# Two weight tiles moved ahead of modulation blocks in the load queue at the start of a two-block transformer kernel

## What is computed

```python
mod = jax.nn.silu(c) @ w_ada[l] + b_ada[l]
sh1, sc1, g1, sh2, sc2, g2 = jnp.split(mod[:, None, :], N_MOD, axis=-1)
u = rmsnorm(h, norm1_w[l]) * (1.0 + sc1) + sh1
proj = u @ w_in[l]
hq, hf, hi, hg, aq, ak, av = jnp.split(proj, offs, axis=-1)
o_hg = hgrn2(hq, hf, hi, hg, lower_bounds[l], hgrn_gnorm_w[l])
lam = (exp(sum(diff_lambda_q1 * diff_lambda_k1)) - exp(sum(diff_lambda_q2 * diff_lambda_k2)) + lambda_init)
o_da = diff_attention(aq, ak, av, lam, lambda_init, diff_subln_w[l])
mix = jnp.concatenate([o_hg, o_da], axis=-1) @ w_out[l]
h = h + g1 * mix
u = rmsnorm(h, norm2_w[l]) * (1.0 + sc2) + sh2
h = h + g2 * ((jax.nn.silu(u @ w_ffn_gate[l]) * (u @ w_ffn_up[l])) @ w_ffn_down[l])
```

## Time and profile before

| what | value |
|---|---|
| median of 3 runs | 1474.66 us |
| the profiled execution | 1473.02 us |
| its span, first to last instruction | 1471.2 us |
| around the span | 1.8 us |
| PE busy, share of the span | 98% |
| DVE busy | 64% |
| ACT busy | 28% |
| granted TensorE clock, mean | 0.991 |

### The profile page before, as it was taken

How to read it: one execution, slowest core, us unless ns; L and a number is a source line. 1 busy time by engine, 2 the same in 40 slices (tenths; PEclk the granted TensorE clock), 3 DMA queues, 4 the chain that set the end, 5 groups by cost and what they waited for, 6 DMA issues and landing times.

```text
span 1471.2 us, 19416 instructions
## 1 busy us (share of the span) xinstructions
PE 1445.6 (98%) x7240; PEld 1174.3 (80%) x7240; DVE 937.3 (64%) x1666; ACT 412.9 (28%) x838; POOL 94.9 (6%) x75
## 2 busy tenths in 40 slices
PE   8999999999999999999999999999999999999997
PEld 7888777778888888888877777788887888888886
DVE  8887797886676665566566668765565444544443
ACT  6335355231111111013345456410122222221011
POOL 0100000200000001225100000000120000000110
PEclk9999999999999999999999999999999999999998
DMA  9444421436556564533221111123322232233332
GB/s 369 183 158 141 146 77 51 149 130 206 187 191 194 186 195 138 159 93 116 74 71 44 44 51 42 46 93 101 101 85 93 93 99 101 86 100 93 95 96 89
DMA packets 52464, 175.26 MB, mean 119 GB/s; under 512 B 5936, under 2 KB 6320, under 8 KB 52400
## 3 DMA queue, kind: packets, MB, share of 16 engines
q1 hardware_dynamic: 52400, 174.41, 36.0%
HBM read 172.29 MB, written 2.10 MB: 119 GB/s over the span
## 4 chain that ended last, share of the span: by engine, by line
PE 91%; DVE 4%; DMA 1%; ACT 1%; issue 1%; SPq 0%; ACTq 0%; DVEq 0%
PE bank L669 20%; PE bank L671 20%; PE bank L670 20%; PE bank L1182 8%; PE bank L1202 2%; PE bank L1237 2%; PE bank L1213 2%; PE bank L1036 2%; PE bank L861 2%; PE bank L863 2%; PE bank L862 2%; DMA fraw<-in_w_in_dram 1%; PE bank L895 1%; PE bank L834 1%; PE bank L835 1%
## 5 line engine op out<-in xcount | busy, mean ns | idle before, releaser
L669 PE MATMUL bank<-uh,wh 128*128 128x512 f32 x808 | 316.7, 392 | 6.1 <-DVE wl L1736 4.5
L670 PE MATMUL bank<-ul,wh 128*128 128x512 f32 x808 | 315.5, 390 | 0.0
L671 PE MATMUL bank<-uh,wl 128*128 128x512 f32 x808 | 315.5, 390 | 0.0
L1734 DVE CAST wh<-wraw 128x1024 fp32r<-128x1024 f32 (+1 forms) x223 | 147.8, 663 | 194.4 <-PE bank L671 178.8
L1736 DVE TENSOR_TENSOR wl<-wraw,wh 128x1024 fp32r<-128x1024 f32 (+1 forms) x223 | 261.4, 1172 | 7.7
L669 PEld LDWEIGHTS bank<-uh,wh 128*128 128x128 f32 x808 | 152.4, 189 | 38.9 <-issue 5.8
L671 PEld LDWEIGHTS bank<-uh,wl 128*128 128x128 f32 x808 | 152.4, 189 | 32.1
L670 PEld LDWEIGHTS bank<-ul,wh 128*128 128x128 f32 x808 | 152.5, 189 | 31.6
L669 PE MATMUL bank<-hh,wh 128*128 128x512 f32 x352 | 137.5, 391 | 0.0
L671 PE MATMUL bank<-hh,wl 128*128 128x512 f32 x352 | 137.0, 389 | 0.0
L670 PE MATMUL bank<-hl,wh 128*128 128x512 f32 x352 | 137.0, 389 | 0.0
(11 more groups left out here) (362 smaller groups left out, 2263.3 us busy)
## 6 DMA issues: line engine op xcount, KB each, us to landing
ada<-in_w_ada_dram SPq DMA_DIRECT2D x94, 512.0 KB, 4.7
wraw<-in_w_in_dram SPq DMA_DIRECT2D x61, 512.0 KB, 3.4
wraw<-in_w_ffn_gate_dram SPq DMA_DIRECT2D x44, 512.0 KB, 3.4
wraw<-in_w_ffn_up_dram SPq DMA_DIRECT2D x44, 512.0 KB, 3.4
wraw<-in_w_ffn_down_dram SPq DMA_DIRECT2D x32, 512.0 KB, 3.5
wraw<-in_w_ffn_down_dram SPq DMA_DIRECT2D x16, 384.0 KB, 3.1
wraw<-in_w_out_dram SPq DMA_DIRECT2D x16, 256.0 KB, 2.7
wraw<-in_w_out_dram SPq DMA_DIRECT2D x8, 512.0 KB, 3.4
```

The lines of the kernel that those rows point to most:

```text
L669: nc.tensor.matmul(bank[:], a, rh[:, k0 + k, :], start=(first and k == 0), stop=False)
L670: nc.tensor.matmul(bank[:], a, rl[:, k0 + k, :], start=False, stop=False)
L671: mm = nc.tensor.matmul(bank[:], b, rh[:, k0 + k, :], start=False, stop=(last and k == nk - 1))
L1734: V.tensor_copy(wh[:, slot, 0:n], wraw[:, slot, 0:n]).then_inc(w_hi, 1)
```

## The change

On SP the eight front units are issued in three groups, two behind the modulation blocks of k = 0, four behind those of k = 1, two behind those of k = 2; the lambda row and the second vector go behind all modulation blocks. On DVE the rests of units 4 and 5 stand at the end of k = 1's rests, those of units 6 and 7 behind `front_low(2)`, in each case ahead of `x_normed` and `front_gain`; the small chains of k = 3 and k = 6 stand behind the level masks, and on both sides of the late modulation blocks. On ACT the exponentials go behind the loop. PE's and POOL's order is unchanged.

```diff
+        FRONT_UNITS = [(0, 1), (2, 3, 4, 5), (6, 7)] + [()] * (KT - 3)
...
             for k in range(KT):
                 load_front_mod(2 * k)
                 load_front_mod(2 * k + 1)
-                if k < FRONT // 2:
-                    load_front_unit(2 * k)
-                    load_front_unit(2 * k + 1)
-                if k == 1:
-                    sp.dma_start(lamv[:].rearrange("p a d -> p (a d)"),
-                                 t_in["lam"].broadcast_to([P, 4 * HD])).then_inc(lam_in, 16)
-                if k == 4:
-                    sp.dma_start(vt2[:], t_in["vec_2"]).then_inc(vec_in, 16)
+                for n in FRONT_UNITS[k]:
+                    load_front_unit(n)
+            sp.dma_start(lamv[:].rearrange("p a d -> p (a d)"),
+                         t_in["lam"].broadcast_to([P, 4 * HD])).then_inc(lam_in, 16)
+            sp.dma_start(vt2[:], t_in["vec_2"]).then_inc(vec_in, 16)
             sp.dma_start(scb[:, 1, :], t_in["c_2"].broadcast_to([P, D])).then_inc(c_land, 16)
...
             for k in range(KT):
-                if k == 5:
-                    act.wait_ge(setup_v, 5)
-                    A(lsc[:, 4:12], lsc[:, 4:12], ACT.Exp)
-                    A(lsc[:, 20:22], lsc[:, 20:22], ACT.Exp).then_inc(setup_a, 1)
...
                 A(uh[:, k, :], tn[:, k % 4], ACT.Copy).then_inc(n_uh, 1)
+            act.wait_ge(setup_v, 5)
+            A(lsc[:, 4:12], lsc[:, 4:12], ACT.Exp)
+            A(lsc[:, 20:22], lsc[:, 20:22], ACT.Exp).then_inc(setup_a, 1)
...
             for k in range(1, KT):
+                if k == 1:
+                    front_rest(2)
+                    front_rest(3)
                 if k < FRONT // 2:
-                    front_rest(2 * k)
-                    front_rest(2 * k + 1)
                     front_low(k)
+                if 0 < k < FRONT // 2 - 1:
+                    front_rest(2 * k + 2)
+                    front_rest(2 * k + 3)
                 for n in (2 * k, 2 * k + 1):
                     if n < KT:
                         x_normed(n)
...
-                if k == 3:
-                    l0, l1 = vt1[:, LB:LB + 4], vt1[:, LB + 4:LB + 8]
...
-                if k == 6:
-                    v.wait_ge(setup_a, 1)
...
             level_masks(range(5, 7))
+            l0, l1 = vt1[:, LB:LB + 4], vt1[:, LB + 4:LB + 8]
...
+            v.wait_ge(lam_in, 16)
...
             for j in range(16, MOD0):
                 late_modulation(j)
+            v.wait_ge(setup_a, 1)
...
             v.wait_ge(mod_done, MOD0)
```

More of the change, by code:

```diff
@@ L1989, in _ @@
-            level_masks(range(5, 7))
+            level_masks(range(5, 7))
+            l0, l1 = vt1[:, LB:LB + 4], vt1[:, LB + 4:LB + 8]
+            link(V.tensor_tensor(lsc[:, 0:4], l0, l1, ALU.max))
+            link(V.tensor_tensor(lsc[:, 4:8], l0, lsc[:, 0:4], ALU.subtract))
+            link(V.tensor_tensor(lsc[:, 8:12], l1, lsc[:, 0:4], ALU.subtract))
+            v.wait_ge(lam_in, 16)
+            for m in range(2):
+                link(V.tensor_tensor_reduce(lamv[:, 2 * m, :], lamv[:, 2 * m, :], lamv[:, 2 * m + 1, :], 1.0, 0.0,
+                                            ALU.mult, ALU.add, lsc[:, 20 + m:21 + m]))
@@ L1990, in _ @@
             for j in range(16, MOD0):
                 late_modulation(j)
+            v.wait_ge(setup_a, 1)
+            link(V.tensor_tensor(lsc[:, 12:16], lsc[:, 4:8], lsc[:, 8:12], ALU.add))
+            link(V.reciprocal(lsc[:, 16:20], lsc[:, 12:16]))
+            link(V.tensor_tensor(lbs, lsc[:, 4:8], lsc[:, 16:20], ALU.mult))
+            link(V.tensor_scalar(oml, lbs, -1.0, 1.0, ALU.mult, ALU.add))
+            link(V.tensor_tensor(lsc[:, 22:23], lsc[:, 20:21], lsc[:, 21:22], ALU.subtract))
@@ L1992, in _ @@
+            link(V.tensor_scalar(nlam, lsc[:, 22:23], LAMBDA_INIT, -1.0, ALU.add, ALU.mult))
             v.wait_ge(mod_done, MOD0)
```

## The result

| | before | after |
|---|---|---|
| median, us | 1473.3 (22 runs, 1470.87 to 1480.75) | 1477.74 (22 runs, 1475.98 to 1479.72) |
| ratio to before | | 1.0028, 95% interval 1.0021 to 1.0034 |
| profiled execution, us | 1473.02 | 1478.43 |
| its span, us | 1471.2 | 1475.9 |

The change makes the kernel 4.1 us slower, 3.1 to 5.0 by the interval.

What follows compares the result with a forecast made beforehand. TensorE, busy 98% of the span, was taken as the bound, with VectorE deciding the front. 1.9 us at unit 7 plus 0.9 for the clock gave +2.8, added to the median: 1477.5 us, range 1472.5 to 1481.0.

Steps and rivals of the forecast that it cites:

- Where the front's delay goes: Front of the kernel: a delay of TensorE there reaches the end almost one to one.
- Units 4 and 5 earlier, the pause goes: Front loads: units 4 and 5 land at 20.2 and 21.4, and TensorE's 2.08 us pause for unit 4's rest goes.
- VectorE stands for 1.6 us behind each gain: VectorE in the front: after the gains of k = 2 and 3 it idles about 1.6 us until `ul` can start.
- +1.9 us at unit 7: TensorE begins unit 7 at 40.7 instead of 38.84, waiting for VectorE's eighth `xn`: +1.9 us.
- +0.9 us for the clock: Low TensorE clock behind the new pause at unit 7: between 0 and 1.7 us, the middle taken, +0.9 us.
- The rest, at nothing: Lambda and lower-bound chains and exponentials moved behind the loop: 0 us, VectorE through at 64.8, hidden by the `forget` wait.
- lambda row too late: Rival behind the loop: ScalarE and VectorE wait for the late-issued lambda row, +8 us or more; chance 0.03.
- Absorbed: Rival: later waits of TensorE, such as those for VectorE, take up the delay, 0 us; chance 0.09.
- no stall: Rival in the front: VectorE's 1.7 us hops are hidden after all and unit 7 begins at 37.3, -1.5 us; chance 0.07.
- Late all the same: Rival: the slow DMA stretch is not the lambda row's, unit 4 is rounded at 24.2, +4.8 us; chance 0.11.
- The possible gain: TensorE's front pause and low clock: 3.8 us at most; VectorE's chain without a stall gives only -1.5 us.

Runs made afterwards that it cites:

- rests back in their places: The changed kernel with VectorE's rests of units 2k and 2k+1 again ahead of the `ul` of k, loads as changed: 1472.52 us, ratio 0.9998.
- half of the column sums: 16 of TensorE's 32 column-sum matmuls left out, as a time probe, in three kernels: before 1471.21 us, changed 1475.65, VectorE in order of need 1470.15.
- filled pauses: The changed kernel with 7 and 14 zero-weight matmuls put into TensorE's two pauses (third `ul`, unit 7): 1475.46 us, ratio 1.0017 to before.
- interleaved order: The changed kernel with VectorE's `xn`, unit rests and gains in the order in which TensorE needs them: 1472.76 us, ratio 1.0001 to before.
- order alone: The kernel before with only VectorE's new order of unit rests; loads, lambda chains and ScalarE as they were: 1480.55 us, ratio 1.0049.

## Why the prediction was right, and where it was off

The predicted 1477.5 us stand against 1477.74 measured, in the range of 1472.5 to 1481.0. The direction and the place were right. But the sum was 2.8 us and the measured difference is 4.1 (3.1 to 5.0). The two errors, the sum and the median of three to which it was added (1.4 us too high), cancelled: that the number came out this near is luck, the place and the way are not.

- *Where the front's delay goes.* Almost one to one to the end, as said. Over all 14 profiles the next phase begins between 65.94 and 77.30 us, and what is left of the span behind that lies between 1401.0 and 1403.2 us.
- *Units 4 and 5 earlier, the pause goes.* Shown. ScalarE rounded unit 4 at 21.92 (forecast 21.35; its work before that was 0.6 us late by the column sums). Unit 4 landed at 21.7, though, not at 20.2: issued at 7.48 and 14.2 us on its way. With ScalarE not free before 21.9 this cost nothing here. With the rests back in their places ScalarE did wait for it, 0.29 us.
- *VectorE stands for 1.6 us behind each gain.* Shown: 1.54 us twice, 0.26 for unit 6 (forecast 0.4). With half of the column sums, where nothing comes late at the start, the changed kernel follows the forecast's times: third gain 28.61 (28.4), third `ul` 30.31 (30.1), end of the eighth `xn` 40.85 (40.7), unit 7 at 40.99 (40.7).
- *+1.9 us at unit 7: too small.* Against that one execution it is right (41.67 - 38.84, less 0.9 for the column sums). The step that failed is the base of 38.84. It was taken from an execution in which TensorE itself was late, by the pause of 2.08 us and the low clock behind it. Without that, before's unit 7 is bound by VectorE too and begins at 38.09. The term is 40.99 - 38.09 = 2.9 us, from one profile of each.
- *+0.9 us for the clock: too small.* The filled pauses give 1.6 us. From unit 7 to the next phase the changed kernel takes 2.7 us more than before (31.9 against 29.2), and 1.6 with half of the column sums (71.97 - 40.99 against 67.45 - 38.09). So the price is near or over the upper end of the 0 to 1.7 that was taken as bounds: around the end of the pause of 3.50 us the clock was low from 40.3 to 47.2 us, behind that of 2.08 only from 29.0 to 32.4. The lower bound rested on one sample too: the pause of 1.97 us at 309 us is in all 14 profiles (1.97 or 1.98 us, ending between 305 and 318), and in 8 of them a low clock follows it, as with the rests back in their places:

```profile
308.14 0.49 PE L667 MATMUL bank<-uh,wh 128*128 128x512 f32 x1 [1.98 <-DVE wl L1733]
```

```profile
309.00:310.00 1.00, 1.00 (x3) 0.78 (x3) 1.00 (x3) 0.00 (x0) 0.00 (x0) 0.50 0.75 213
```

The sum by the corrected terms is 2.9 + 1.6 = 4.5 us, where 4.4 was measured with half of the column sums.
- *The rest, at nothing.* Shown: VectorE was through at 65.5 (forecast 64.8), the `forget` waited 4.33 us, the lambda row went out at 38.3 and landed 6.1 us later. The rival with the lambda row too late is out.
- *The rivals.* Absorbed and no stall are out by the profile. "Late all the same" is out as to its cause: the slow stretch left with the lambda row. Some of the lateness did stay, 1.5 us in the profile of the change (21.7 against 20.2). The 1.95 us by which the prediction has VectorE later in this case is a slip for 1.8 (24.2 against 22.4), without weight. The rule that spoke for this rival, that transfers from 512 B per descriptor run at line rate (the Trainium skill, DMA: Bandwidth & Descriptors, Specifications), does not hold for this row, which one 1 KB source sends to 128 partitions: 134 to 176 GB/s in its slow stretch, in the four profiles that have the row at this place of the queue, and 393 to 430 between 18 and 20 us in the ten without it.
- *The possible gain.* The prediction gave 3.8 us as the most that this place could give and then 1.5 as the best case of VectorE's chain. The second was the right measure: with half of the column sums the interleaved order begins unit 7 1.5 us earlier (36.58 against 38.09), and 1.1 us of it showed in the time, with overlapping intervals. That the two figures are equal is in part luck, since the forecast's 1.5 was against 38.84. With the full sums no gain was measured.

## What to carry to other kernels

An engine that waits for a late load may sit on a second bound just behind it: sum the other engine's work up to the next meeting point before taking the wait for a gain. When work is moved out from between a producer's last step and its consumer on an in-order queue, ask what it was lying over: here two unit rests hid 1.7 us of another engine, and moving them cost about 4 us, while the early load by itself gave nothing that could be measured. A pause in one profile is one sample: a second profile of the same kernel showed 0.76 us where the first had 2.08.

## What was not expected of the hardware

TensorE's 32 one-column matmuls (128 x 128 weights each) took between 3.71 and 6.99 us, by how much of them fell in a low-clock stretch, and the engine that waits for them starts up to 3.6 us late (with the order alone). What TensorE did before those stretches was small work: 128-column and one-column matmuls. The length of a pause alone did not decide on the clock behind it: the pauses of 1.80, 1.82 and 1.86 us for the third `ul` brought no low clock, that of 1.88 us at unit 7 with half of the column sums did, and that of 1.97 us near 309 us did in 8 of 14 profiles. The one of 3.50 us did in both profiles of the change, and the same place did not with the pause filled. And unit 4 landed 2.8 us behind unit 3 in the changed kernel (21.67 and 18.91), where its bytes take 1.25 us and the DMA engines ran at 393 GB/s or more. All ten profiles without the lambda row at this place have at least one such late landing, 1.9 to 2.8 us behind the one before it, of unit 4, unit 5 or a modulation block; why is open.
